# A gated MLP as seven block products per tile, and its down projection moved behind it

## The reference

```
h = rmsnorm(x, norm2_w) * (1.0 + sc2) + sh2
gate, up = split(causal_dwconv(h @ w_up, conv_ff_w), 2)     # width-3 convolution over tokens
x = x + gt2 * ((silu(gate) * up) @ w_down)
return rmsnorm(x, norm_f_w)
```

## Time and profile before

| | |
|---|---|
| Median of 3 runs | 1527.27 us |
| Span of the profiled execution | 1523.0 us |
| Mean granted TensorE clock over the span | 0.965 |
| PE busy | 1427.9 us (94%), 7019 matmuls |
| DVE busy | 674.3 us (44%) |
| POOL busy | 624.9 us (41%) |
| ACT busy | 452.2 us (30%) |
| The chain that ended last | PE 81%, DVE 8%, ACT 5% |

### The profile page before, as it was taken

The page is one execution under the profiler, slowest core; times in us unless marked ns, Lnnn a source line. Parts: engine busy times, 40 slices in busy tenths (PEclk is TensorE's granted clock), DMA queues, the critical chain, the costliest instruction groups (busy, mean ns, idle before and its releaser), DMA issues.

```text
span 1523.0 us, 18439 instructions
## 1 busy us (share of the span) xinstructions
PE 1427.9 (94%) x7019; PEld 1191.1 (78%) x7019; DVE 674.3 (44%) x857; ACT 452.2 (30%) x516; POOL 624.9 (41%) x359
## 2 busy tenths in 40 slices
PE   3899999999979999889979999999999999999996
PEld 3477878878768999876858888888888888888884
DVE  3825152342656666435553343424243342343426
ACT  3326345351722222133323131221212122131223
POOL 4357667586724111114335252433425234252430
PEclk8799999999989999979989999999999999999998
DMA  8043424233110001101102111111201112111102
GB/s 334 16 125 95 106 56 130 69 89 90 55 56 1 1 0 55 56 28 40 58 0 71 41 56 41 41 41 51 73 28 55 41 41 69 41 55 41 41 28 111
DMA packets 122348, 92.36 MB, mean 61 GB/s; under 512 B 3903, under 2 KB 110668, under 8 KB 122316
## 3 DMA queue, kind: packets, MB, share of 16 engines
q1 hardware_dynamic: 122316, 91.94, 20.0%
HBM read 87.73 MB, written 4.19 MB: 60 GB/s over the span
## 4 chain that ended last, share of the span: by engine, by line
PE 81%; DVE 8%; ACT 5%; issue 3%; DMA 2%; POOL 1%; SPq 0%; POOLq 0%; DVEq 0%; ACTq 0%
PE ps L1497 22%; PE ps L1499 22%; PE ps L1498 22%; PE ps L1623 5%; PE ps L1642 3%; PE ps L1639 2%; DVE sq_lo L1190 1%; DMA ada_first<-in_ada_w_dram 1%; PE ps L1529 1%; DVE ada_first L1103 1%; DVE sq L1187 1%; DVE x L1477 1%; DMA x_hi<-in_x_dram 1%; ACT sq L832 1%; ACT L832 1%
## 5 line engine op out<-in xcount | busy, mean ns | idle before, releaser
L1497 PE MATMUL ps<-h,w_split 128*128 128x512 f32 x448 | 177.4, 396 | 0.0
L1498 PE MATMUL ps<-h,w_split 128*128 128x512 f32 x448 | 176.8, 395 | 0.0
L1499 PE MATMUL ps<-h,w_split 128*128 128x512 f32 x448 | 176.7, 394 | 0.0
L1168 DVE SCALAR_TENSOR_TENSOR cu<-ps,col_c,cu 128x1023 f32<-128x1023 f32 (+1 forms) x44 | 56.4, 1282 | 217.2 <-ACT cu L827 214.3
L1455 DVE TENSOR_TENSOR x<-x,ps 128x512 f32<-128x512 f32 x160 | 107.2, 685 | 76.9 <-PE ps L1499 76.9
L1497 PE MATMUL ps<-wd_split,act_split 128*128 128x512 f32 x352 | 137.9, 392 | 3.2 <-POOL act_split L750 3.2
L1497 PE MATMUL ps<-h,wg_split 128*128 128x512 f32 x352 | 137.8, 391 | 2.2 <-POOL h L623 2.2
L1499 PE MATMUL ps<-wd_split,act_split 128*128 128x512 f32 x352 | 137.7, 391 | 0.0
L1498 PE MATMUL ps<-wd_split,act_split 128*128 128x512 f32 x352 | 137.5, 391 | 0.0
L1499 PE MATMUL ps<-h,wg_split 128*128 128x512 f32 x352 | 137.4, 390 | 0.0
L1498 PE MATMUL ps<-h,wg_split 128*128 128x512 f32 x352 | 137.4, 390 | 0.0
(11 more groups left out here) (272 smaller groups left out, 2811.4 us busy)
## 6 DMA issues: line engine op xcount, KB each, us to landing
ada_raw<-in_ada_w_dram SPq DMA_DIRECT2D x32, 512.0 KB, 4.0
w_raw<-in_w_in_dram SPq DMA_DIRECT2D x28, 512.0 KB, 5.2
wg_raw<-in_w_up_dram SPq DMA_DIRECT2D x22, 512.0 KB, 5.0
wu_raw<-in_w_up_dram SPq DMA_DIRECT2D x22, 512.0 KB, 3.8
wd_raw<-in_w_down_dram SPq DMA_DIRECT2D x22, 512.0 KB, 3.3
ada_first<-in_ada_w_dram SPq DMA_DIRECT2D x4, 2048.0 KB, 17.4
x<-in_x_dram SPq DMA_DIRECT2D x4, 1024.0 KB, 5.9
out_dram<-x SPq DMA_DIRECT2D x8, 512.0 KB, 2.6
```

Source lines behind the costliest of these rows:

```text
L1168: dve.scalar_tensor_tensor(out=dst[:, lag:L], in0=src[:, 0:L - lag], scalar=weight, in1=dst[:, lag:L], op0=ALU.mult, op1=ALU.add).then_inc ...
L1497: pe.matmul(dst, a_hi, b_hi, start=(first and n == 0), stop=False)
L1498: pe.matmul(dst, a_hi, b_lo, start=False, stop=False)
L1499: mm = pe.matmul(dst, a_lo, b_hi, start=False, stop=(last and n == len(pairs) - 1))
```

## The change

The hidden tiles are computed with seven block products instead of eight (Strassen's scheme in Winograd's form). For a tile f the four operand blocks of weights are the gate and the up columns, each for the first and the second half of the 1024 input channels (g0, g1, u0, u1), and the blocks of h are its token halves by its channel halves. A product takes 4 blocks of 128 input channels and 512 tokens: 12 matmuls. So a tile has 7 x 12 = 84 matmuls, where it had 96. The sums that the scheme needs are made as follows.

- Of the weights, each tile: `sum_w` on DVE, four sums of 128x512 (u0+u1 and so on); ACT then makes seven high parts and POOL seven low parts of 128x512, in place of two of 128x1024 each. The raw weights of a tile are one 1 MB buffer, refilled when all seven are split.
- Of h, once: `late_sums` on DVE, six operations of 128x512 for each of the token tiles 4 to 7, and five instead of two parts of such a tile to split. The scaling to `xn2` goes from DVE to ACT.
- Of the products: four are accumulated in PSUM on top of another (P2 on P1, P7 and P4 on P6, P3 on P5), and DVE and ACT take the sums out between them (`keep_p1`, `keep_u2`, `keep_u3`, `take_c11`, `take_c22`, `take_c12`, `take_c21`) into the SBUF tensors `gs` and `us`. The convolution's taps now read these and not PSUM.

The hidden activations are stored to a DRAM tensor (22 stores of 512 KB). The down projection comes after all 22 tiles: 44 steps, first 22 for tokens 0 to 511, then 22 for the rest. A step loads 512 KB of down weights and 256 KB of activations, DVE multiplies the weights by the gate row, ACT and POOL split both, and PE does 8 output tiles of 3 matmuls. The sums stay in the 8 banks over 22 steps, so that DVE adds to x2 16 times in place of 176. There are two raw buffers and a ring of six split ones. The last four steps are done output tile by output tile. All loops over f and over steps are written out.

More of the change, by code:

```diff
@@ L588, in _ @@
+            for tt in range(TH, TT):
+                store_out(tt)
             sp.wait_ge(s.out_done, 16 * TT)
@@ new lines, in _, with keep_p1, take_c11 @@
+            up_top(0, 6)
+            norm2_stage(TT - 1)
+            for op in (5, 7, 3, 4):
+                up_top(0, op)
+            def keep_p1(f):
+                wait(s.prod_mm, product_done(f, 1))
+                if f:
+                    wait(s.cu_conv, f)
+                else:
+                    wait(s.out_mm, 4 * TT)
+                act.activation(us[:, 0:BANK], bank(f_bank(f, 0)), ACT.Copy).then_inc(s.p1_kept, 1)
+            def take_c11(f):
+                wait(s.prod_mm, product_done(f, 2))
+                if f:
+                    wait(s.cg_conv, f)
+                act.activation(gs[:, 0:BANK], bank(f_bank(f, 0)), ACT.Copy).then_inc(s.c11_out, 1)
@@ L1063, in _ @@
                 act.activation(rstd[:, tt:tt + 1], var[:, tt:tt + 1], ACT.Sqrt).then_inc(s.norm_rstd, 1)
+            for n in range(2, STEPS):
+                down_top(n)
+                if n >= FT + 4 and n < FT + 4 + TH:
+                    final_square(n - FT - 4)
+            for tt in range(TH, TT):
+                final_square(tt)
         @block.vector
@@ L1473, in final_rows, with drain_down @@
+            for f in range(FT):
+                mlp_tile(f)
+            def drain_down(n):
+                tt, half = n // 2, n % 2
+                dve.wait_ge(s.down_tile_mm, n + 1)
+                piece = x2[:, tt, half * BANK:(half + 1) * BANK]
+                dve.tensor_tensor(piece, piece, bank(n % 8), ALU.add).then_inc(s.x2_mlp, 1)
             def final_rows(tt):
@@ new lines, in _, with down_tile @@
+            for f in range(FT):
+                mlp_tile(f)
+            def down_tile(n, tile, first, last):
+                slot, toks = n % RING, slice(tile // 2 * P, (tile // 2 + 1) * P)
+                cols = slice(tile % 2 * BANK, (tile % 2 + 1) * BANK)
+                return three_pass(bank(tile), [(ad_split[slot][:, 0, toks], ad_split[slot][:, 1, toks],
+                                                wd_split[slot][:, 0, cols], wd_split[slot][:, 1, cols])],
+                                  first=first, last=last)
```

654 lines of the change are left out of this document (400 added, 254 removed).

## The result

The changed kernel took 1531.10 us, the median of 7 runs (1530.09 to 1532.45), beside 1524.57 us of the kernel before in 7 runs (1521.89 to 1528.35). The ratio is 1.0037, with a 95% interval of 1.0025 to 1.005: it is slower by 0.4%, where 0.4% faster was forecast. The time lies within the stated range; the sign is wrong. (The forecast was made against 1527.27 us, the median of the first 3 runs of the kernel before. Against its median of 7, the forecast's 1521.5 us is 0.2% faster.) The profiled execution has a span of 1529.2 us, against 1523.0 before and 1517 in the forecast.

A forecast was written before the change was run, and what follows sets the result against it. The prediction took PE to set the time, the other engines covered by it. Its terms summed to -7.9 us, taken as -6: span 1517, time 1521.5 us, range 1492 to 1562 us.

The forecast's parts named there:

- The wait before P7: Hidden tiles: PE idles 1.1 us per tile until DVE's chain reaches `keep_u2`; +23 us over 21 tiles.
- The clock's rival: Hidden tiles: PE's gap drops its clock to half, 1.7 us lost in each of 21 tiles; +36, 1557 us; chance 0.22.
- The stores to DRAM: Hidden tiles: 22 activation stores of 512 KB are hidden beside 19 us of matmuls each; no cost.
- one wait of 13.5 (14.3) before the last group: Last four down steps: all four buffers are needed before the first matmul; +14.3 us.
- The end: After PE's last matmul: half the rows finish early, leaving 7.8 us against 11.8; -4.0 us.
- The port: DVE operations with two SBUF operands and POOL's exclude each other; a tap beside a split took 3.14 us, not 1.28.
- The first tile product after the norm: Norm to tile 0: DVE's sums and POOL's splits share the port, P2 starts near 807, not 791.7; +15.4 us.
- The count of matmuls: Hidden tiles: 12 fewer matmuls in each of 22 tiles, 264 at 0.2265 us; -59.8 us.
- The matmul pitch: All matmuls: time per matmul stays 0.2265 us; rival of longer matmuls, at 5% +21, 1542 us; chance 0.05.
- The gate row and DVE's wait for the second tile's weights: First tiles: gate row's matmuls between P7 and P3 of tile 0, +1.8; DVE waiting for weights, +0.6 us.
- that leaves `take_c22` 0.3 us before P3: Hidden tile: weights landing 5.7 us after issue leave `take_c22` this margin before P3; 0.1 us added per tile.
- The halves: Change of halves in the down phase: DVE is in step 24's gate row when the first drain is wanted; +1.2 us.

The follow-up runs named there:

- e9: Changed kernel with e7's order, next gate weights loaded after four splits and sum 3, only the up weights after the seventh split: 1505.49 us, ratio 0.9875.
- e3: Changed kernel with POOL splitting only 4 of 128 columns for products 6, 3 and 4 in tiles 1 to 21: 1505.36 us, ratio 0.9879.
- e1: Changed kernel with P1 kept in its own buffer and the next tile's `keep_u2` between the two taps of cu: 1531.73 us, ratio 1.0043.
- e7: Changed kernel with e1's edit, and `keep_u3` and `take_c22` ahead of all weight sums on DVE: 1523.58 us, ratio 0.9991.
- e2: Changed kernel with e1's edit, and `keep_u3` and `take_c22` behind sum 5, ahead of sums 6 and 7: 1521.20 us, ratio 0.9972.
- e10: Changed kernel with its own order on DVE and ACT, only the gate weights loaded early as in e9: 1527.37 us, ratio 1.0019.

## Why the prediction went wrong

**What held.** That the matmuls taken out are 60 us and the question is whether the other engines stay covered. The wait before P7: 1.1 us a tile, forecast and measured, with taps of 1.72 and 2.26 us for the forecast "near 1.9". The clock's rival did not come: waits of 0.8 us left it at 1.00. The stores to DRAM were hidden, as forecast (e9). Down steps at PE's own 5.44 us, with one wait of 13.5 (14.3) before the last group. The end at -4.2.

**The port.** e3 shows it: the taps' median is 1716 ns beside POOL's full splits and 1280 ns where three of the seven splits are 4 columns of 128. The Trainium skill ("SBUF — State Buffer", Who interferes with whom) says that a DVE instruction with two SBUF inputs contends with a GpSimd instruction that reads SBUF, over a port pair that is an exclusive lock; these two medians agree with it.

**What failed is the sum, by many terms of one sign.** It gave -7.9 us and +6.2 were measured. Seven of the nine came out worse than forecast, by some 15 us together, and two better, by 1.1. No single one turns the sign. By size:

- The first tile product after the norm, "+15.4", was +18.5. The working was not followed to its end: 757.4 + 4 + 48.4 is 809.8, with ACT's last high parts still to come, where the forecast wrote "near 807". 809.8 gives +18.1. P2 was measured at 810.13, but 1.4 us of that is scatter ahead of the changed part; without it the term is +17.1. So the term failed by 1.7 us, and the layout that it came from would have been 1.0 off the other way; that 809.8 lies so near to 810.13 is luck.
- The count of matmuls. "P1 done as 24 gate matmuls were done before" treats 12 as 24: P1 lies in the old wait, but before, 24 were hidden there. 252 and not 264 came off what follows, +2.7.
- The matmul pitch, for which the forecast had 0 and a rival of 5%: 2.3 us over 2892 matmuls, 0.35%. A longer pitch is at most 0.6 of it: e9's tiles take 19.04 us for 84 matmuls, 0.2267 each, and the down steps 5.44 for 24. Some of the rest may be the few slower starts behind each wait; it was not followed.
- The gate row and DVE's wait for the second tile's weights, +1.8 and +0.6, were 4.5, and two later waits for `take_c22`, 2.2, had no term. Both are one oversight: "that leaves `take_c22` 0.3 us before P3" priced as +0.1. That was the mark of a second closed ring. It was treated as a margin, while a margin of 0.3 us in a ring is gone wherever the ring starts late: in the first two tiles, at one in the middle, and in this execution in the last.
- The halves, "+1.2", were 3.5. The gate row of step 24 waited 2.65 us for its load and then took 1.96 us beside POOL's split; the forecast had DVE busy in it, and no wait for the load. The additions that PE waits for stand behind it:

```profile
1381.80 1.96 DVE L1769 TENSOR_TENSOR wd_raw<-wd_raw,gate_row 128x1024 f32<-128x1024 f32 x1 [2.65 <-DMA wd_raw<-in_w_down_dram]
...
1383.68 4.86 DVE L1805 TENSOR_TENSOR x<-x,ps 128x512 f32<-128x512 f32 x8
```

**A reading of the clock that holds for one execution only.** The forecast's rival took from the earlier trace rows that waits of about 2 us bring half clock. The same wait of PE, 2.12 us at 309 us, brought 0.62 in the kernel before and left the clock at 1.00 in the changed one:

```profile
308.76 0.50 PE L1929 MATMUL ps<-sq_hi,ones_r 128*128 128x512 f32 x1 [2.12 <-DVE sq_lo L1435]
...
309.00:313.00 4.00, 4.00 (x19) 1.00 0.08 18
```

So the rows could not place a wait of 1.1 us between "full" and "half", and its chance of 0.22 rested on less than it seemed. The forecast also puts PE at half clock for "below half" of 1494 to 1498; the mean of 0.57 makes that some 3.4 of the 4 us. Its price for it, 1.7 us, fits the 3.4.

**What the forecast had in hand but not in its number.** It took one chain for the tile and added what it cost. There were three rings within 0.4 us of one another (median tiles of 20.17 us through DVE's convolution in the changed kernel, 20.03 through P3 and the load in e1, 19.8 through the load and POOL alone in e7). e1, e2, e7 and e10 each open one or two and win at most 6.5 us; e9 opens all and wins 23.8. For the size of the change this made no difference, for what to do about it all the difference.

## What to carry to other kernels

Where a buffer is refilled only after its last reader, write down the whole ring (load, readers, what they wait for) and its length beside PE's time for the same round; a ring that is nearly as long has no margin, however idle the engines in it look. When a wait is taken away and the time stays, look for the wait that took its place and follow it to its own ring. A change that takes much off the bounding engine and adds waits at every transition (start, first round, middle, last round) should have a term for each of them, since they all have the same sign.
